# The prompt's path up to W_out interleaved into the sample steps of a straight program

## What is computed

```python
h = _rmsnorm(x, g_pre_mix)
z = h @ w_in + b_in
q, k, v, cva, cvg = jnp.split(z, [D_ATTN, 2 * D_ATTN, 3 * D_ATTN, 3 * D_ATTN + D_CV], axis=-1)
...
attn = moba_fn(q, k, v)
glu = cva * jax.nn.sigmoid(cvg)
glu_ext = jnp.concatenate([cv_hist, glu], axis=1)
c = _causal_dwconv(glu_ext, w_cv_dw, b_cv_dw)
c = jax.nn.silu(_layernorm(c, g_cv_ln, b_cv_ln))
c = c @ w_cv_pw + b_cv_pw
mix = jnp.concatenate([attn, c], axis=-1) @ w_out
x = x + _rmsnorm(mix, g_post_mix)
h = _rmsnorm(x, g_pre_ffn)
u = h @ w_up
u_ext = jnp.concatenate([ffn_hist, u], axis=1)
u = _causal_dwconv(u_ext, w_ffn_dw, b_ffn_dw)
gate, val = jnp.split(u, 2, axis=-1)
f = (jax.nn.silu(gate) * val) @ w_down
x = x + _rmsnorm(f, g_post_ffn)
```

## Time and profile before

| | us |
|---|---|
| median of 3 runs (1157.41 to 1162.14) | 1161.44 |
| profiled execution, its time | 1158.29 |
| its span, first to last instruction | 1156.5 |
| TensorE busy | 970.9 |
| DVE busy | 650.9 |
| POOL busy | 584.5 |
| ACT busy | 372.0 |

### The profile page before, as it was taken

One profiled execution on the slowest core, in us unless ns is written; L12 is line 12 of the kernel. 1 busy time (PEld: TensorE's weight loads), 2 busy tenths in 40 slices (PEclk: granted clock), 3 DMA queues, 4 the chain that ended last, 5 costly groups with the idle time before them and its releaser, 6 DMA issues.

```text
span 1156.5 us, 21529 instructions
## 1 busy us (share of the span) xinstructions
PE 970.9 (84%) x7656; PEld 742.5 (64%) x7656; DVE 650.9 (56%) x1009; ACT 372.0 (32%) x683; POOL 584.5 (51%) x534
## 2 busy tenths in 40 slices
PE   4988676776767676778899989999999997999995
PEld 3856464545343534355464449999999997777773
DVE  3478595867798988625712335545554557423114
ACT  3123131313130313234432224433443442134223
POOL 2002999999999994003301115565555563133443
PEclk9999696979787778899899998999999999999998
DMA  9787999999989899971043002223322320222232
GB/s 319 279 277 256 318 319 317 335 323 308 322 287 324 289 317 335 313 239 43 1 164 102 8 1 73 74 73 90 91 73 73 105 77 1 91 73 73 73 87 82
DMA packets 150949, 202.40 MB, mean 175 GB/s; under 512 B 9985, under 2 KB 71426, under 8 KB 150864
## 3 DMA queue, kind: packets, MB, share of 16 engines
q1 hardware_dynamic: 149078, 197.68, 52.4%
q10 hardware_dynamic: 1828, 4.17, 1.1%
HBM read 196.49 MB, written 5.68 MB: 175 GB/s over the span
## 4 chain that ended last, share of the span: by engine, by line
PE 61%; SPq 14%; DVE 9%; issue 6%; DMA 5%; ACT 3%; ACTq 1%; POOL 0%; POOLq 0%; DVEq 0%
SPq L323 10%; PE tp L765 6%; PE z L765 6%; PE sc L765 6%; PE z L812 5%; PE z L741 4%; DMA B<-in_cache_k 3%; PE ob L765 3%; PE sm L765 3%; PE z L470 3%; PE sc L812 3%; PE tp L812 3%; PE sc L741 2%; SPq L313 2%; PE sc L504 2%
## 5 line engine op out<-in xcount | busy, mean ns | idle before, releaser
L1560 POOL TENSOR_SCALAR A<-A,consts 128x512 f32<-128x512 f32 x93 | 150.5, 1618 | 110.9 <-DVE A L1308 101.8
L1202 DVE STREAM_TRANSPOSE B<-B 128x2048 f32<-128x2048 f32 x64 | 144.7, 2291 | 48.1 <-DMA B<-in_cache_k 46.9
L1581 POOL TENSOR_TENSOR wulo<-B,wuhi 128x2048 fp32r<-128x2048 f32 x22 | 108.6, 4938 | 91.5 <-ACT wuhi L1070 64.5
L1563 POOL TENSOR_TENSOR A<-A 128x576 f32<-128x576 f32 x90 | 128.9, 1432 | 7.5
L556 PE MATMUL ob<-B 128*32 128x128 f32 x2048 | 81.9, 321 | 45.2 <-DMA B<-in_cache_v 44.2
L1624 POOL TENSOR_TENSOR wdlo<-B,wdhi 128x1024 fp32r<-128x1024 f32 x22 | 60.0, 2730 | 97.9 <-ACT wdhi L1137 97.9
L556 PEld LDWEIGHTS ob<-B 128*32 128x32 f32 x2048 | 67.7, 147 | 58.5 <-DMA B<-in_cache_v 55.1
L1453 DVE TENSOR_TENSOR fTlo<-A,fThi 128x1152 fp32r<-128x1152 f32 x22 | 32.0, 1455 | 105.6 <-ACT fThi L1136 101.4
L1465 DVE TENSOR_SCALAR B<-B,small 128x512 f32<-128x512 f32 x44 | 25.3, 575 | 115.9 <-ACT B L1108 115.9
L504 PE MATMUL sc<-B,A 128*32 128x256 f32 x1024 | 73.6, 449 | 4.5 <-DVE B L1202 3.9
L1468 DVE SCALAR_TENSOR_TENSOR B<-B,small 128x512 f32<-128x512 f32 x88 | 66.2, 752 | 3.1
(11 more groups left out here) (317 smaller groups left out, 2558.0 us busy)
## 6 DMA issues: line engine op xcount, KB each, us to landing
B<-in_cache_k SPq DMA_DIRECT2D x256, 256.0 KB, 4.8
B<-in_cache_v SPq DMA_DIRECT2D x256, 256.0 KB, 3.9
B<-in_w_up SPq DMA_DIRECT2D x44, 512.0 KB, 4.9
B<-in_w_down SPq DMA_DIRECT2D x22, 512.0 KB, 3.7
B<-in_w_in SPq DMA_DIRECT2D x16, 512.0 KB, 7.2
B<-in_w_in SPq DMA_DIRECT2D x3, 2048.0 KB, 16.7
B<-in_w_out SPq DMA_DIRECT2D x1, 4096.0 KB, 13.9
B<-in_x_prompt SPq DMA_DIRECT2D x4, 512.0 KB, 8.9
```

What stands on the lines that cost most here:

```text
L1202: dve.transpose(kT[:, u % 4, :, :].rearrange("p c (i k) -> p i c k", i=4), kN[:, u % 4, :, :].rearrange("p i (c k) -> p i c k", k=32)).the ...
L1560: pool.tensor_scalar(dst[:, 0:TP_], glu[:, i, j:j + TP_], w, b2, *bias)
L1563: ins = pool.tensor_tensor(conv[:, i, :], conv[:, i, :], prod, ALU.add)
L1581: pool.tensor_tensor(wulo[:, slot, :, :], wu[slot].rearrange("p k u n -> p k (u n)"), wuhi[slot][:, :, :].bitcast(F32), ALU.subtract).then ...
```

## The change

The eight steps are written out without engine loops, as are the up and the down projection. SBUF is laid out anew, all in one region: K gets three chunk buffers instead of four, wz two instead of one, q of the prompt is held without zero padding, the probabilities of a head take 1280 columns instead of 2048. Into the steps go, by the function `fill(b, u)` of each engine, called after chunk u of step b, and by code ahead of first_values: two glu tiles in each of steps 0 and 1, two tiles of v and k in each of steps 2 and 3; the rows of k and v and their stores ahead of step 4's values; four heads in each of steps 4 and 5, their normalising on POOL; the statistics ahead of the values of steps 5 and 6; the LayerNorm's tail and the pointwise product ahead of step 6's values; W_out of tiles 0 and 1 in step 6, of tile 2 ahead of step 7's values and of tile 3 in its chunks; tile 4 behind the first two groups of the up projection. The convolution's products are made on ACT (two instructions a tap into one of two buffers), two taps after each chunk of step 0, four after each chunk of steps 1 to 3 and four ahead of the exponentials of steps 1 to 3; POOL adds them up. The squares of x1's rows move from ACT to DVE. The load of gFfn is awaited ahead of the first rest of the gated rows. The diff's core (the loops of TensorE that go; then SP's new order, TensorE's fill and steps, ACT's taps, POOL's sums and normalising):

```diff
-            scores(0, (0, 1))
-            with pe.Fori(0, 4) as i:
-                scores(i, (2, 3))
-                glu_tiles(i)
-                pe.wait_ge(s["ot_put"], i + START)
-                first_values(i)
-                scores(i + 1, (0, 1))
-                last_values(i)
-            with pe.Fori(0, 3) as i:
-                scores(i + 4, (2, 3))
-                kv_tiles(i)
-                first_values(i + 4)
-                scores(i + 5, (0, 1))
-                last_values(i + 4)
-            scores(7, (2, 3))
-            kv_tiles(3)
-            first_values(7)
-            last_values(7, kN)
...
+            load_k(0)
+            load_k(1)
+            sp.dma_start(wv[:, :, :], w_in[:, :, 2 * DA:3 * DA]).then_inc(s["wv_loaded"], 16)
+            for c in range(2, 8):
+                load_k(c)
+            sp.wait_ge(s["ks_done"], 1)
+            load_wz(0)
+            load_wz(1)
+            sp.wait_ge(s["zq_done"], 2 * HP)
+            for b in range(NB):
+                if 1 <= b <= 3:
+                    load_wz(2 * b + 1)
+                for u in range(4):
+                    load_v(8 * b + u)
+                if b == 6:
+                    sp.wait_ge(s["pv2_done"], H)
+                    sp.wait_ge(s["stored_cv"], 64)
+                    sp.dma_start(wo[:, :, :], a["w_out"][0].rearrange("(k p) n -> p k n", p=P)).then_inc(s["wo_loaded"], 16)
+                    sp.wait_ge(s["stored_v"], 16)
+                    sp.dma_start(gPost[:, :], a["g_post_mix"][0].partition_broadcast(P)).then_inc(s["gpost_loaded"], 16)
+                if b < NB - 1:
+                    for u in range(3):
+                        load_k(8 * b + 8 + u)
+                if b < 3:
+                    load_wz(2 * b + 2)
+                if b == 6:
+                    sp.wait_ge(s["pw_done"], 2 * CT)
+                    for t in range(2):
+                        sp.dma_start(x1[t][:, :], a["x_prompt"][0, t * P:(t + 1) * P, :]).then_inc(s["xa_loaded"], 16)
+                if b == 7:
+                    sp.wait_ge(s["pw_put"], 2 * CT)
+                    for t in range(2, 4):
+                        sp.dma_start(x1[t][:, :], a["x_prompt"][0, t * P:(t + 1) * P, :]).then_inc(s["xb_loaded"], 16)
+                    sp.dma_start(x1[4][0:TS, :], a["x_sample"].rearrange("b t n -> (b t) n")).then_inc(s["xb_loaded"], 16)
                     sp.wait_ge(s["kt_ready"], NB * SUPER)
+                    sp.dma_start(histF[0:16, :], a["state_ffn"][0].rearrange("b w n -> (b w) n")).then_inc(s["histf_loaded"], 16)
+                for u in range(4, 8):
+                    if b < NB - 1:
+                        load_k(8 * b + 7 + u)
+                    load_v(8 * b + u)
+                if b < NB - 1:
+                    load_k(8 * b + 15)
+                if b == 5:
+                    sp.wait_ge(s["conv_done"], CT)
+                    sp.wait_ge(s["glun_done"], 2)
+                    sp.dma_start(wpw[:, :, :], a["w_cv_pw"][0].rearrange("(k p) n -> p k n", p=P)).then_inc(s["wpw_loaded"], 16)
...
+            def fill(b, u):
+                if b in (0, 1) and u % 2:
+                    glu_group(2 * b + 1, u // 2)
+                if b in (2, 3):
+                    i = 2 * b - 3
+                    if u == 0:
+                        value_tile(i)
+                    elif u == 3:
+                        turn_values(i, b, False)
+                    elif u == 4:
+                        key_tile(i)
+                if b in HEADS_AT:
+                    h = HEADS_AT[b]
+                    if u == 0:
+                        pe.wait_ge(s["pto_put"], b + 1)
+                        pe.wait_ge(s["mask_put"], 1)
+                        if b == 5:
+                            pe.wait_ge(s["mu_put"], 2)
+                        s_head(h)
+                    elif u == 1:
+                        s_head(h + 1)
+                    elif u == 2:
+                        t_head(h)
+                    elif u == 3:
+                        pv_head(h)
+                        s_head(h + 2)
+                    elif u == 4:
+                        t_head(h + 1)
+                    elif u == 5:
+                        pv_head(h + 1)
+                        s_head(h + 3)
+                    elif u == 6:
+                        t_head(h + 2)
+                    else:
+                        pv_head(h + 2)
+                        t_head(h + 3)
+                        pv_head(h + 3)
+                if b == 6:
+                    if u == 0:
+                        pe.wait_ge(s["wo_loaded"], 16)
+                        pe.wait_ge(s["pw_put"], 2 * CT)
+                    mix_half(u // 4, u // 2 % 2, u % 2)
+                if b == 7:
+                    if u < 2:
+                        h2_tile(u)
+                    elif u < 6:
+                        mix_half(3, u // 2 - 1, u % 2)
+                    elif u == 6:
+                        h2_tile(2)
...
+            for b in range(NB):
+                scores(b, 2)
+                if b:
+                    turn_out(b - 1)
+                scores(b, 3)
+                if b in (0, 1):
+                    for n in range(4):
+                        glu_group(2 * b, n)
+                if b in (2, 3):
+                    value_tile(2 * b - 4)
+                    key_tile(2 * b - 4)
+                    turn_values(2 * b - 4, b, True)
+                if b == 4:
+                    rows_out()
+                if b == 5:
+                    pe.wait_ge(s["o2_put"], 2)
+                    statistics(conv, s["st1_done"], s["conv_done"], CT)
+                if b == 6:
+                    statistics(sq, s["st2_done"], s["sq_ready"], 1)
+                    pe.wait_ge(s["sd_put"], 2)
+                    pe.wait_ge(s["wpw_loaded"], 16)
+                    pe.wait_ge(s["c_ready"], 1)
+                    for n in range(2 * CT):
+                        pointwise(n)
+                if b == 7:
+                    for n in range(4):
+                        mix_half(2, n // 2, n % 2)
+                    turn_history()
+                if b in (2, 3):
+                    pe.wait_ge(s["v2_home"], 2 * b - 3)
+                if b == 7:
+                    pe.wait_ge(s["hf_put"], 2)
+                first_values(b)
+                for u in range(SUPER):
+                    weigh(b, u)
+                    fill(b, u)
+                    if b < NB - 1 and u in (2, 5):
+                        scores(b + 1, u // 3)
+            turn_out(NB - 1)
...
+            def taps(count):
+                for n in range(tap["n"], min(tap["n"] + count, CT * CW)):
+                    i, j = n // CW, n % CW
+                    if j == 0:
+                        act.wait_ge(s["z1_put"], 2 * i + 2)
+                        if i == 0:
+                            act.wait_ge(s["glu_clear"], 1)
+                            act.wait_ge(s["hist_put"], 2)
+                    if n >= 2:
+                        act.wait_ge(s["prod_used"], n - 1)
+                    dst = prod[:, n % 2, :]
+                    gx = glu[:, i, GX:GLUW].rearrange("p (b x) -> p b x", b=NB)
+                    act.activation(dst[:, 0:TP_], glu[:, i, j:j + TP_], ACT.Copy, scale=w_cv[:, i, j:j + 1])
+                    act.activation(dst[:, TP_:TOK].rearrange("p (b t) -> p b t", b=NB), gx[:, :, j:j + NT], ACT.Copy,
+                                   scale=w_cv[:, i, j:j + 1]).then_inc(s["prod_put"], 1)
+                tap["n"] = min(tap["n"] + count, CT * CW)
...
+            for n in range(CT * CW):
+                i, j = n // CW, n % CW
+                pool.wait_ge(s["prod_put"], n + 1)
+                if j == 0:
+                    pool.tensor_scalar(conv[:, i, :], prod[:, n % 2, :], w_cv[:, i, CW:CW + 1], None, ALU.add).then_inc(s["prod_used"], 1)
+                else:
+                    pool.wait_ge(s["prod_used"], n)
+                    ins = pool.tensor_tensor(conv[:, i, :], conv[:, i, :], prod[:, n % 2, :], ALU.add).then_inc(s["prod_used"], 1)
+                if j == CW - 1:
+                    pool.wait_ge(s["prod_used"], n + 1)
+                    pool.sem_inc(s["conv_done"], 1)
+            def normalize(h):
+                j = 4 * (h % 2)
+                pool.wait_ge(s["prr_ready"], h + 1)
+                for t in range(4):
+                    n = (t + 1) * P
+                    row = pP[:, h % 2, tri(t):tri(t) + n]
+                    pool.tensor_scalar(row, row, prr[:, j + t:j + t + 1], None, ALU.mult).then_inc(s["pnorm"], 1)
...
```

1785 lines of the change are left out of this document (862 added, 923 removed).

## The result

The changed kernel takes 1211.92 us (median of 4 runs, 1210.20 to 1222.05), the kernel before 1161.79 us beside it: a ratio of 1.0455, 95% interval 1.0390 to 1.0521. The forecast was 1180 us, in a range of 1105 to 1230. The sign and the range held; the loss is 50 us where 19 were forecast.

A forecast was written before the change was run, and what follows sets the result against it. Page transfers were taken to set the sample steps, with slack on TensorE. The terms 143 + 213 + 140 + 109 + 386 + 187 = 1178, plus 1.8 between span and time, gave 1180 us, range 1105 to 1230.

The forecast's parts named there:

- Step 6: Sample step with the LayerNorm's serial tail, pointwise product and two W_out tiles: 109 us, twice the present step.
- the whole stretch from step 6's end to the up projection's end: Step 7, W_out tiles 2 to 4 and the up projection: 386 us, 139 less than the present kernel.
- the rest: Down projection and end, unchanged but for gFfn's wait: 187 us.
- step 0: Start and first sample step: chunk 7 late by 3 to 6 us; +12, ending at 143 us (bounds 131 and 148).
- Step 1: First of three steps with convolution taps, POOL setting the pace: 71 us (67 to 77), DMA busy well under 0.9.
- gFfn's late load: Between up and down projections: the first rest of the gated rows waits for gFfn, +5 us (0 to 8).
- the openings: Steps 1 to 3, from scaled output to first value product: 24 us each (bounds 20 and 30).
- the openings of steps 4 and 5: Ahead of the value products in the steps with four heads each: 20.5 us of each step's 70.
- The loops: From first value product to the next scaled output: 47 us in steps 1 to 3, 49.5 in steps 4 and 5.
- Transfers: Rival, chance 0.26: page transfers keep setting the steps, saving 39 + 26 us in steps 1 to 5; 1115 us.
- Loop edges: Rival, chance 0.04: engine loops cost stalls that a straight program is rid of, at most 74 us; 1106 us.
- The low clock: Rival, chance 0.20: TensorE's granted clock stays near 0.8 in steps 4 to 7, +42 us; 1222 us.

The follow-up runs named there:

- ln_early: Changed kernel with the LayerNorm's second statistic and its tail moved from step 6 into step 5, the squares in a home of their own: 1198.32 us, ratio 1.0338.
- combined: Changed kernel with taps moved to ACT's waits, LayerNorm in step 5, stores on SP, W_out ahead of the up groups, gFfn awaited at first use: 1145.75 us.
- no_taps: Changed kernel without 116 of the 124 convolution taps on ACT and POOL, output not the reference's: 1167.79 us, ratio 1.0065 to the kernel before.
- order: Changed kernel with the same 124 taps moved out of the openings, 31 in the loop of each of steps 0 to 3: 1215.84 us.
- stores_sp: Changed kernel with the seven stores of key, value and state rows issued on SP instead of ACT: 1224.47 us, ratio 1.0544.
- combined kernels: The combined version with stores on SP (1145.75 us), on ACT (1138.83), on POOL (1136.04), and on POOL with 26 unread products in step 4's opening (1136.74).
- late_home: Changed kernel with TensorE's wait for the turned values in steps 2 and 3 moved ahead of the bank's next use: 1211.36 us.
- warm: Changed kernel with 36 to 48 unread TensorE products in each opening of steps 2 to 5: 1213.76 us, median of three runs.
- before_straight: The kernel before with all its engine loops written out as straight programs, nothing else changed: 1157.99 us, ratio 0.9982.
- warm4: Changed kernel with 26 unread TensorE products in step 4's opening only, ahead of the wait for the rows' evictions: 1216.92 us.
- combined_warm: The combined kernel with its stores on POOL, plus 26 unread TensorE products in step 4's opening: 1136.74 us.
- dve_tile: Changed kernel with the fourth convolution tile's taps on DVE, two behind each chunk of steps 2 and 3: 1210.49 us.

## Why the prediction was off

**What held.** Step 6 (its serial tail shown by ln_early), the whole stretch from step 6's end to the up projection's end (387.1 against 386: step 7 takes 60.8 where 60.5 were forecast, the first dense up group starts 70.4 us behind its end where 69 were), and the rest (188.0 against 187). The number of step 0 held too (144.1 against 143), but in part by luck: chunk 7's transpose was to be 3 to 6 us late and starts at 81.05 where it started at 78.75, and the last thing ahead of the step's end is a glu group of 4.1 us behind the last value chunk, which the forecast did not name. Step 1 (69.4 against 71) comes out by two errors, an opening that is longer and a loop that is shorter, and its transfers are still busy 0.95 and 0.90, where well under 0.9 was to be seen from step 1 on. In the rest, gFfn's late load is seen as forecast:

```profile
1036.64 2.63 DVE L1538 TENSOR_TENSOR fTlo<-fT,fThi 128x1152 fp32r<-128x1152 f32 x2 [4.19 <-DMA gFfn<-in_g_post_ffn]
...
1038.15 0.76 PE L845 MATMUL z<-wdhi,fThi 128*128 128x512 f32 x1 [14.64 <-DVE fTlo L1538]
```

DVE waits 4.19 us for it, and TensorE 14.64 us between the projections where it waited 6.87 before. In combined, where the load is awaited at its first use, the rest takes 184.0.

**The step that failed: the openings.** The forecast gave those of steps 1 to 3 24 us, bounds 20 and 30: a value between the 20 of the parts alone and the 29.8 of the present stretch with two tiles in it. The four taps ahead of the exponentials were named in it, but got no time of their own. In steps 2 and 3, which measured 31.7 and 31.6, they have it. In step 2 the key tile's eviction starts 18.7 us behind the output, since both tiles come first on TensorE; 1.1 us of evictions follow, then the four taps, 4.9 us at POOL's pace; and from the exponentials to the first value product it is 7.0. The tiles alone already fill the 24: without taps these openings take 25.4 and 25.2 us (no_taps), with taps in the loops only 27.5 and 27.9 (order). The forecast also put the taps of the last chunk into the loop alone. They hold the next step's first eviction for 6.7 us, where it comes 1.1 us behind the output without taps, but in steps 2 and 3 the ranking that they delay still ends with the tiles, so there they cost next to nothing.

For the openings of steps 4 and 5 the forecast took 20.5 us. Step 4 has no tile in its opening, and there the taps left from step 3 do cost: they hold the eviction for 7.6 us. Behind the ranking ACT still issues stores, and its exponentials start 2.2 us behind the last penalty, where the stores were said to end when the ranking does. With the taps out of the way the opening is 24.2 to 26.0 us (order, no_taps), so 2.8 to 4.6 of the 8.3 us are the taps; the rest is put down to the rows and stores, which stores_sp could not take apart, as its step waited for a key chunk instead. In step 5 the 3.5 us are a cost that the forecast had at nothing: POOL's subtraction of the mean runs beside DVE's ranking. A row of DVE and POOL's:

```profile
464.91 4.31 DVE L1321 TENSOR_SCALAR small<-small 128x32 f32<-128x32 f32 x1
...
464.14 5.03 POOL L1633 TENSOR_TENSOR conv<-conv,mu 128x2304 f32<-128x2304 f32 x1 [13.51 <-ACT mu L1127]
```

An instruction of 32 columns, 0.18 us elsewhere, takes 4.31 us until POOL's 5.03 us are over. In the combined kernels the subtraction waits for the ranking, and this opening is 19 to 20 us.

**The loops.** POOL's pace was right: an add each 1.54 us where 1.50 was taken. The loops of steps 1 to 3 measured 44.1 to 49.6 where 47 were forecast, though four of their 32 taps still follow the output that ends them here; about 4 us in each of steps 2 and 3 are TensorE's and ACT's mutual wait for the turned values (late_home). Step 4's loop misses by 4, and that is the clock: at 0.96 it takes 48 us (order, warm), where the forecast had 49.5.

**The rivals.** Transfers do not set steps 2 to 5; without the taps they come near to it (no_taps). Loop edges cost nothing that can be told (before_straight). The low clock's condition held in step 4 alone (0.75; 0.86 to 0.90 in steps 5 to 7), and there it cost some 5 us in the loop, not the 42 of four steps. What it costs in the total stays open: warm4 and combined_warm raised it in step 4, and their totals did not fall. Nor was it tried whether a fourth key buffer or more product buffers help.

**The rule on POOL.** By the figure of the Trainium skill, GPSIMD Engine Reference, section Performance versus the Vector engine, an add of 576 columns was estimated at 1.25 us and three steps at 189; the adds take 1.54 us back to back, and the row's 1.50 was the better choice.

## What to carry over

When work is moved into another engine's program, list for every instruction already there what now stands ahead of it, the tail of the previous round included, and then ask which of the things it needs comes last. The same kind of delay was free in steps 2 and 3, where two tiles took as long, and cost several us in step 4, where no tile stood; the four taps between the key tile's eviction and the exponentials cost their whole 4.9 us. Taking one wait of a ring away moves the time to the next; what helped was to place the work where its engine waits anyway, and to see who is held up by it there. A queue that carries the loads of the next step is no place for a store that waits.

## What the runs showed of the hardware

Beside POOL's work DVE is held up far more than the forecast allowed, which priced both as if alone: DVE's tap 1.02 us alone and 2.37 beside POOL's adds, a pair of subtractions 0.76 and 3.05, an instruction of 32 columns 0.18 and 4.31. POOL hardly shows it: its adds take 1.41 us each in step 2 of the changed kernel and 1.46 beside DVE's taps in dve_tile. The Trainium skill, SBUF — State Buffer, section SBUF: two separate sides, says that these two engines share a pair of ports under a lock, which DVE needs for an instruction in a two-port mode or with two SBUF inputs; the one that starts first holds it for a whole instruction, while the other stands still. The row of 4.31 us, which ends with POOL's subtraction, agrees with that; in which mode its instruction of 32 columns ran, no run here shows.

The granted clock differs between executions of the same instructions: step 5's loop had 0.79, 0.82, 0.93 and 0.97 in the four combined kernels, and took 55.6, 55.1, 49.0 and 48.9 us.

Issuing a store took ACT 0.4 to 2.3 us: the seven take 8.0 us of ACT in order and 10.4 in no_taps from the first to the last, with two evictions among them.
